# Three-part products with the rest last, and two more pairs by seven products, in a two-block transformer kernel on one core

## The reference

```
x = x + mix @ w_out
h = rmsnorm(x, norm_mlp);  x = x + square(relu(h @ w_up)) @ w_down      # w_up 1024x4096
x = rmsnorm(x, norm_final)
h = rmsnorm_2(x, norm_mix_2);  proj = h @ w_in_2                        # second block
...
g, u = split(n @ w_ffn_in, 2);  x = x + (silu(g) * u) @ w_ffn_out       # hidden width 2816
```

## Time and profile before

| | |
|---|---|
| median of 3 runs | 953.79 us (952.92 to 955.75) |
| the profiled execution's own time | 953.05 us |
| its span, first to last instruction | 951.2 us |
| busy: TensorE, VectorE, ScalarE, GpSimd | 942.7, 705.6, 560.0, 131.5 us |
| TensorE's mean granted clock | 0.998 of full speed |
| moved by DMA | 170.45 MB |

### The profile page before, as it was taken

The page is one execution under the profiler, slowest core; times in us unless marked ns, Lnnn a source line. Parts: engine busy times, 40 slices in busy tenths (PEclk is TensorE's granted clock), DMA queues, the critical chain, the costliest instruction groups (busy, mean ns, idle before and its releaser), DMA issues. The chain is left out here.

```text
span 951.2 us, 17011 instructions
## 1 busy us (share of the span) xinstructions
PE 942.7 (99%) x6898; PEld 868.1 (91%) x6898; DVE 705.6 (74%) x939; ACT 560.0 (59%) x854; POOL 131.5 (14%) x181
## 2 busy tenths in 40 slices
PE   9999999999999999999999999999999999999997
PEld 7877899989999999989987999998998899999996
DVE  6767875778877887878866787776666467777777
ACT  6577554557666666666865674545455445555544
POOL 2100001005223320414000001100000012121210
PEclk9999999999999999999999999999999999999999
DMA  9974447555666666656565365555655346565661
GB/s 305 307 244 128 119 128 174 165 178 175 201 192 193 193 195 198 183 162 199 146 187 163 104 200 178 172 185 172 198 161 170 118 156 204 173 200 178 201 198 67
DMA packets 133552, 170.45 MB, mean 179 GB/s; under 512 B 5825, under 2 KB 97297, under 8 KB 133473
## 3 DMA queue, kind: packets, MB, share of 16 engines
q1 hardware_dynamic: 131408, 165.07, 57.2%
q10 hardware_dynamic: 1424, 2.84, 0.8%
q0 software_dynamic: 640, 1.44, 0.7%
HBM read 168.28 MB, written 1.05 MB: 178 GB/s over the span
## 5 line engine op out<-in xcount | busy, mean ns | idle before, releaser
L1668 DVE TENSOR_TENSOR parts<-raws,parts 128x1024 fp32r<-128x1024 f32 (+3 forms) x307 | 364.6, 1203 | 126.7 <-ACT parts L1115 125.9
L1115 ACT ACTIVATE parts<-raws 128x1024 fp32r<-128x1024 f32 (+3 forms) x307 | 309.1, 1029 | 126.4 <-PE ps L405 52.4
L403 PE MATMUL ps<-room_r,parts 128*128 128x256 f32 x1248 | 351.5, 282 | 0.0
L404 PE MATMUL ps<-room_r,parts 128*128 128x256 f32 x1248 | 348.6, 279 | 0.0
L405 PE MATMUL ps<-room_r,parts 128*128 128x256 f32 x1248 | 348.3, 279 | 0.0
L403 PEld LDWEIGHTS ps<-room_r,parts 128*128 128x128 f32 x1248 | 234.6, 188 | 2.3 <-issue 0.8
L404 PEld LDWEIGHTS ps<-room_r,parts 128*128 128x128 f32 x1248 | 234.7, 188 | 1.2
L405 PEld LDWEIGHTS ps<-room_r,parts 128*128 128x128 f32 x1248 | 234.6, 188 | 0.0
L434 PE MATMUL ps<-parts,room_r 128*128 128x512 f32 (+1 forms) x336 | 134.0, 399 | 1.0 <-DVE parts L1668 1.0
L436 PE MATMUL ps<-parts,room_r 128*128 128x512 f32 (+1 forms) x336 | 131.1, 390 | 0.0
L435 PE MATMUL ps<-parts,room_r 128*128 128x512 f32 (+1 forms) x336 | 131.1, 390 | 0.0
(11 more groups left out here) (243 smaller groups left out, 1118.4 us busy)
## 6 DMA issues: line engine op xcount, KB each, us to landing
raws<-in_w_in SPq DMA_DIRECT2D x99, 512.0 KB, 4.5
raws<-in_w_ffn_in SPq DMA_DIRECT2D x44, 512.0 KB, 4.6
raws<-in_w_up SPq DMA_DIRECT2D x32, 512.0 KB, 3.9
raws<-in_w_down SPq DMA_DIRECT2D x32, 512.0 KB, 3.8
raws<-in_w_ffn_out SPq DMA_DIRECT2D x22, 512.0 KB, 4.4
raws<-in_w_xkv SPq DMA_DIRECT2D x16, 512.0 KB, 4.1
raws<-in_w_out SPq DMA_DIRECT2D x8, 512.0 KB, 4.2
raws<-in_w_up_ssd SPq DMA_DIRECT2D x8, 512.0 KB, 5.5
```

What stands on the lines that cost most here:

```text
L403: e.matmul(ps, wh, hT[0][:, k, :], start=k == 0, stop=False)
L404: e.matmul(ps, wh, hT[1][:, k, :], start=False, stop=False)
L1115: e.activation(t.h, t.raw, ACT.Copy).then_inc(s["hi"], 1)
L1668: e.tensor_tensor(t.l, t.raw, t.h.bitcast(F32), ALU.subtract).then_inc(s["lo"], 1)
```

## The change

Four edits:

1. In `fm`, `tm`, `lead` and `down` the two products with a tile's rounded part come first, for all k of the tile, behind a wait for `hi`; the product with the tile's rest comes last, behind a wait for `lo`. In `down_by_sums` the same holds for the weights and for the sums tile.
2. The first tile of all (`early`) is taken factor by factor, each with its own wait.
3. `by_sums` takes in q=14 of MLP and q=0 of the gated stage.
4. In the gated stage ScalarE makes more tiles ahead of Silu for q=1 and 2, and the parts of the sums for q=0 and 1 come at the end of the turn in place of its start (VectorE too).

```
-        by_sums = [range(14), range(1, 10)]
+        by_sums = [range(15), range(10)]
...
-                        for k in range(K):
-                            t = own[k // 4]
+                        for k0, t in zip(range(0, K, 4), own):
+                            ks = range(k0, k0 + 4)
+                            need(s["hi"], t.i + 1)
+                            for k in ks:
+                                ready(k)
+                                wh = t.h[:, k - k0, c:c + P]
+                                e.matmul(ps, wh, hT[0][:, k, :], start=k == 0, stop=False)
+                                e.matmul(ps, wh, hT[1][:, k, :], start=False, stop=False)
                             need(s["lo"], t.i + 1)
-                            ready(k)
-                            wh, wl = (v[:, k % 4, c:c + P] for v in (t.h, t.l))
-                            e.matmul(ps, wh, hT[0][:, k, :], start=k == 0, stop=False)
-                            e.matmul(ps, wh, hT[1][:, k, :], start=False, stop=False)
-                            last = e.matmul(ps, wl, hT[0][:, k, :], start=False, stop=k == K - 1)
+                            for k in ks:
+                                last = e.matmul(ps, t.l[:, k - k0, c:c + P], hT[0][:, k, :], start=False, stop=k == K - 1)
...
+                        need(s["hi"], w_.i + 1)
+                        if early:
+                            need(s["xT_hi"], 1)
+                            product(0, 0, w_.h, True)
+                            need(s["xT"], 1)
+                            product(0, 1, w_.h)
+                            need(s["xT_hi"], 2)
+                            product(1, 0, w_.h, True)
+                            need(s["lo"], w_.i + 1)
+                            product(0, 0, w_.l)
+                            product(1, 0, w_.l)
+                            need(s["xT"], 2)
+                            last = product(1, 1, w_.h)
+                            early = False
...
-                    need(s["lo"], w_.i + 1)
+                    need(s["hi"], w_.i + 1)
                     product(p1, u11, w11, first)
                     product(c11, u12, w21, first and q == 0)
                     need(s["usT"], nth_sums[u][q] + 1)
-                    w_.release = done(product(c12, s4, w22))
+                    product(c12, s4, w22)
+                    need(s["lo"], w_.i + 1)
+                    with_rest(p1, u11, w11)
+                    with_rest(c11, u12, w21)
+                    w_.release = done(with_rest(c12, s4, w22))
+                    need(s["hi"], sums.i + 1)
+                    product(p6, s2, t2, first)
+                    product(p5, s1, t1)
+                    product(p7, s3, t3)
+                    product(c21, u22, t4, first and q == 0)
                     need(s["lo"], sums.i + 1)
...
             for q in range(11):
-                until(where["gate", q].at)
-                sums_rounded(1, q - 1)
+                until(where["gate", q].at + (q in (1, 2)))
+                if q > 2:
+                    sums_rounded(1, q - 1)
                 full(("gate", q))
```

More of the change, by code:

```diff
@@ L412, in fm, with tm @@
                     yield
-            def tm(name, w, c0, cn, hT, ready, ahead=False, first=0, depths=None):
+            def tm(name, w, c0, cn, hT, ready, ahead=False, first=0, depths=None, early=False):
                 K = w.shape[0] // P
@@ L427, in tm @@
                         asked = None
-                        need(s["lo"], w_.i + 1)
[L429 to L438, removed]
+                        ks = range(k0, k0 + deep)
@@ new lines, in product @@
+                        def product(t, of, part, begins=False, ends_=False):
+                            for k in ks:
+                                if not early:
+                                    ready(k, t)
+                                last = e.matmul(psum[:, own[t], 0:nb], hT[of][:, k, t * P:t * P + P], part[:, k - k0, :],
+                                                start=begins and k == 0, stop=ends_ and k == K - 1)
+                            return last
+                        need(s["hi"], w_.i + 1)
@@ new lines, in tm @@
+                        if early:
[11 more added lines that the diff above has]
+                            early = False
+                        elif next_deep:
+                            for t in range(2):
+                                product(t, 0, w_.h, True)
+                                product(t, 1, w_.h)
+                            need(s["lo"], w_.i + 1)
+                            for t in range(2):
+                                last = product(t, 0, w_.l)
+                        else:
+                            for t in range(2):
+                                product(t, 0, w_.h, True)
+                                product(t, 1, w_.h)
+                                need(s["lo"], w_.i + 1)
+                                ends(product(t, 0, w_.l, False, True), (name, b0 // 512, t), own[t])
@@ L574, in tensor @@
             w_in = a["w_in"][0]
[L575 removed]
+            units = tm("qkv", w_in, 0, 512, xT, x_ready(MIX), depths=[1, 1, 2, 2, 2], early=True)
             next(units)
@@ L760, in mlp, with product, with_rest @@
                 sums_in = {}
[L762 to L765, removed]
+                def product(ps, left, right, first=False):
+                    e.matmul(ps, left[0], right[0], start=first, stop=False)
+                    e.matmul(ps, left[1], right[0], start=False, stop=False)
+                def with_rest(ps, left, right, over=False):
+                    return e.matmul(ps, left[0], right[1], start=False, stop=over)
                 def down_by_sums(q):
```

61 lines of the change are left out of this document (41 added, 20 removed).

## The result

The changed kernel takes 954.86 us (median of 22 runs, 954.33 to 955.20), the kernel before in runs beside it 953.46 (952.78 to 955.75). The ratio is 1.0013, with a 95% interval of 1.0008 to 1.0019: 1.2 us slower by the ratio (1.4 by the medians), within the 0.3% called no change. The forecast was 954.6. The profiled execution took 955.0, its span is 952.8.

The account below looks back on a forecast made before the run. It took TensorE's fixed-pace stream of matmuls as the bound, so only fewer columns or start waits gain. 953.05 less 0.14, less 0.60, plus 2.15 gave 954.46; forecast 954.6 us, range 952.2 to 956.4.

Parts of the forecast that it names:

- The sum: Whole kernel: 953.05 less 0.14, less 0.60, plus 2.15 gives 954.46 us; 954.6 given as forecast, chance 0.66.
- Rest last, in general: All tiles' products: reordering gains nothing where tiles are long ready, and the added satisfied waits cost 0.
- The upper bound of 4.0 us: Rival, all reordered products: 335 added waits cost 0.012 us each, 4.0 more, 958.6 us; chance 0.03.
- First tile: Kernel start: first product 0.8 us earlier, taken back at 14.75 by VectorE's rests of x; 0.14 us gain remains.
- rival (b): Start: the first tile's 0.7 us stays because the fourth tile's load comes earlier; 954.0 us, chance 0.05.
- Two more groups by sums: MLP's q=14 and the gated stage's q=0: each half takes 2.49 us for 2.79, gaining 0.30, together 0.60.
- Cover in the gated stage: Gated stage, up of q=2: VectorE's idle 1.71 us covers the added sums' work; cost 0, without cover 1.5 us.
- The end of MLP: MLP's last transposes: four tile rests ahead of the join make TensorE wait for VectorE's additions, +2.15 us.
- Rival (c): End of MLP: the load of tile (15,1) lands late and delays the join; 956.7 us, chance 0.05.
- Rival (d): End of MLP: waits throw TensorE back to half clock, about 2.35 us more; 956.9 us, chance 0.04.

Follow-up runs that it names:

- 10: Changed kernel with only rest products last and the gated stage's moved tiles; first tile not by factors, sums as before: 953.07 us, ratio 0.9997 to the kernel before.
- 7: Changed kernel with x's second half rounded and rested ahead of the fourth tile at the start: 955.21 us, ratio 1.0018 to the kernel before.
- 1: Changed kernel without MLP's q=14 by seven products: 952.73 us, ratio 0.9993 to the kernel before.
- 6: Changed kernel with one of four tile rests moved behind MLP's join and another behind the second additions: 953.13 us, ratio 1.0001 to the kernel before.
- 11: Kernel before with the gated stage's first pair by seven products too, and no tile moved ahead of Silu: 956.59 us, ratio 1.0034.
- 12: Kernel before with the gated stage's first pair by seven products and ScalarE's tiles ahead of Silu for q=1 and 2: 953.76 us, ratio 1.0005.
- 3: Kernel before with VectorE resting two later tiles ahead of MLP's join, no sums added: 954.42 us, ratio 1.0012.
- 4: Changed kernel with two tile rests and two roundings moved from ahead of MLP's join and its copy to behind them: 956.44 us, ratio 1.0035 to the kernel before.
- 5: Changed kernel with one tile rest and one rounding moved behind MLP's join and its copy: 953.66 us, ratio 1.0001 to the kernel before.
- 8: Changed kernel without q=14 by sums, x's second half ahead of the fourth tile, one 12-matmul unit ahead of the first window product: 952.13 us, ratio 0.9988 to before.
- experiment 9: Changed kernel without q=14 by sums, with x's second half ahead of the fourth tile at the start: 952.98 us, ratio 0.9997 to the kernel before.

## Why the prediction was right, step by step

- **The sum.** 954.46 from the profiled execution; that of the change took 955.0. Its span grew by 1.6, where the sum says 1.41; another 0.35 lies outside the span (2.2 around it in place of 1.85). The right size rests on the steps below, of which one was right for a reason that fell and one is smaller than what executions differ by; in so far it is luck.
- **Rest last, in general: 0.** Shown by 10, but for the 0.10 gained at 555: the list of waits, from which I took that TensorE waits for a rest only at the first tile, leaves out waits that short. The upper bound of 4.0 us, from a spacing that also held other effects, was never near.
- **First tile: -0.14.** The first product started 0.85 earlier (0.8 expected) and 14.67 was 0.08 earlier (0.14), for the reason given. But 7 showed that the step behind it was incomplete: I named 14.75 as the only place of taking back, and rival (b) held that an earlier fourth tile would leave 0.7 to the end. A second one can stand at 57, and in the change's profiled execution it took back what was left. That is not so in every execution: in those of 1 and 6, with the same start as the change, TensorE is 0.30 and 0.41 ahead of before from the windows up to 373, and the first product over windows begins without a wait, in 1 and then in 6:

```profile
56.80 1.93 PE L631 MATMUL ps<-room 128*32 128x256 f32 x32
```

```profile
56.70 1.93 PE L631 MATMUL ps<-room 128*32 128x256 f32 x32
```

  The term is smaller than the scatter. The matmul of 14.75 begins between 14.48 and 14.85 in the five traces that have the start of before, and between 14.30 and 14.67 in the five that have that of the change. So no single pair of traces sizes it.
- **Two more groups by sums: -0.30 each.** The sums of q=14 take 2.49, from 373.60 to 376.09, in place of 2.79, and the gated stage gave 0.31.
- **Cover in the gated stage: 0, else 1.5.** The value held in the change and the reason was wrong. VectorE's idle 1.71 us covers nothing (11), the moved tiles do (12). Without them the price was 3.6 (the measured 3.27 and the 0.30 gained), not 1.5: of the 3.2 us of work 3.0 went into the delay of the tile rests (796.39 to 799.41), and the half clock was added. This is the step that failed.
- **The end of MLP: +2.15.** Forecast and found: join 379.4 and 379.55, additions 382.3 and 382.44, transposes 383.1 and 383.25. The loss, against a run-through 0.31 ahead of before, is 1.57 at the first transposes, 0.28 between the two first pairs and 0.38 at the second pair, 2.2 together. That it is the order, 3, 4 and 5 show; that the rests also drive loads, 4.
- **Rival (c), a late load,** did not come about in the change. Its mechanism, a rest that comes late and a load behind it, did in 4, with a tile of the next stage.
- **Rival (d), the clock.** In the change the row of granted clock stays at 1.00 behind the wait of 1.40, and matmuls keep their pace. But the mechanism is real in this kernel: see 11. The Trainium skill's page "TensorE: Matmul & The Clock Gate", section on the HAM clock gate, says that TensorE's clock goes to half after it idles. Experiment 11 agrees in so far as the fall came behind a stop and is gone in 12 together with the stop, though the granted clock fell only 0.9 us after TensorE had started again. The profiled execution of 4, with a longer stop and no fall, does not agree: a stop alone does not bring it about. In 11 the half clock cost 1.56, from +1.59 to +3.15; (d) had 2.35.

## What to carry to other kernels

An idle stretch is spare time only if what ends it does not itself wait for the work in front of it: follow the releaser back one loop before you book cover. Where an instruction also frees a buffer, moving it behind something moves a load, and the bill comes two queues further on. And a gain at the start is worth nothing until you have looked for the next place where another engine's schedule holds TensorE: in 7 it was gone 42 us on, in 8 it reached the end. Before you give such a gain a size, see how far executions with the same start lie apart.

## What the hardware showed that I had not expected

- A stop of 1.98 us was followed by half clock (0.50 from about 801.6 to 805, experiment 11), one of 2.74 (experiment 4) by none in the profiled execution: there the granted clock is 1.00 in every window from 385 to 402, and matmuls of 256 columns come every 0.117 from 391.56 on. The rows do not say what made the difference. It may lie in the execution and not in the kernel: two of the five executions of experiment 4 took 957.39 and 957.58 us at a mean granted clock of 0.996, the other three 956.10 to 956.44 at 0.999. No trace of those two is kept, so that the clock fell behind the same stop there is likely, not shown.
- One execution of experiment 9's kernel, of eleven, took 3292.95 us. Its profile has TensorE busy for 3284.1 of 3290.8, with matmuls of 512 columns every 0.84 us through most of the span in place of 0.233 and those of 256 every 0.42 in place of 0.117. VectorE's and ScalarE's busy times, 727.6 and 579.7, are near those of the other runs. The granted clock tells nothing here: the page of this execution has no row for it, and the 1.00 in the windows of this trace stands there without a record. Nor does it at the start of the kernel before, where the windows say 1.00 as well, although the matmuls of 128 columns came at half of their later pace. Where no clock is recorded, the spacing of starts still shows that matmuls are slow. The cause is open.

```profile
1499.07 4.51 PE L437 MATMUL ps<-parts,room_r 128*128 128x512 f32 x5
```
